# Turned value sums, softmax rows divided on ScalarE, and no turning step for the outputs, in a hybrid attention and expert layer

## The reference

```python
n = rms_norm(x)                                # width 1024
fq, fk, fv, ff, sq, sk, sv, ga, gb = split(n @ w_in)
# forgetting attention, 8 heads of 64: softmax(q.k/8 + C[t] - C[s]), s <= t
p = softmax(where(valid, s, MASK));  o_fox = p @ fv
# stick-breaking attention, 8 heads of 64, s < t, in log space
a = exp(log_sigmoid(z) + tail);      o_sb = a @ sv
merged = sigmoid(ga) * (o_fox @ w_o_fox) + sigmoid(gb) * (o_sb @ w_o_sb)
h = x + merged @ w_out
out = h + peer_ffn(rms_norm(h))                # 8 heads x 16 experts for a row
```

## Time and profile before

| | before |
|---|---|
| median of 3 runs | 4224.8 us (4221.11 to 4228.86) |
| profiled execution, span | 4221.9 us |
| TensorE busy | 3201.1 us, 76% |
| VectorE busy | 2854.8 us, 68% |
| GpSimd busy | 1367.6 us, 32% |
| ScalarE busy | 1198.4 us, 28% |
| moved by DMA | 1367.21 MB, mean 324 GB/s |

### The profile page before, as it was taken

How to read it: one execution, slowest core, us unless ns; L and a number is a source line. 1 busy time by engine, 2 the same in 40 slices (tenths; PEclk the granted TensorE clock), 3 DMA queues, 4 the chain that set the end, 5 groups by cost and what they waited for, 6 DMA issues and landing times.

```text
span 4221.9 us, 32194 instructions
## 1 busy us (share of the span) xinstructions
PE 3201.1 (76%) x9766; PEld 1661.7 (39%) x9766; DVE 2854.8 (68%) x5552; ACT 1198.4 (28%) x2584; POOL 1367.6 (32%) x1086
## 2 busy tenths in 40 slices
PE   6989918869887677859887759997586677768565
PEld 3345613325445333425454424554262233334222
DVE  2012285778767966768766978886889767467865
ACT  1223102126521112126631116664111245111100
POOL 0000011444433322433333324443434333434463
PEclk9976959878888878978888878998798788878777
DMA  3422346999999958998989888999999888999997
GB/s 122 138 69 102 113 174 229 401 401 384 382 401 380 369 198 304 410 373 353 345 359 392 316 301 347 379 386 383 380 398 364 302 333 339 400 418 384 383 419 324
DMA packets 296027, 1367.21 MB, mean 324 GB/s; under 512 B 36056, under 2 KB 96624, under 8 KB 149392
## 3 DMA queue, kind: packets, MB, share of 16 engines
q0 software_dynamic: 154464, 1116.02, 66.1%
q1 hardware_dynamic: 110480, 222.78, 14.8%
q10 hardware_dynamic: 30912, 26.35, 1.9%
HBM read 1329.52 MB, written 35.10 MB: 323 GB/s over the span
## 4 chain that ended last, share of the span: by engine, by line
DVE 22%; DMA 12%; PE 11%; ACT 5%; issue 5%; SPq 2%; POOL 1%; ACTq 0%; DVEq 0%; POOLq 0%
DVE uv L1365 10%; DMA uv<-expert_uv,rows_u 8%; PE pv L796 5%; DVE held L1388 2%; SPq L537 2%; DVE arena L1356 1%; PE pb L906 1%; DMA uv<-expert_uv,rows_pk 1%; DMA arena<-scratch_gates 1%; POOL uv L699 1%; PE pb L854 1%; PE pb L749 1%; ACT L1140 1%; PE pb L879 1%; DVE arena L1426 1%
## 5 line engine op out<-in xcount | busy, mean ns | idle before, releaser
L699 POOL DMA_INDIRECT uv<-expert_uv,rows_u x1024 | 1311.7, 1281 | 2203.1 <-PE pv L796 1225.8
L796 PE MATMUL pv<-uv,diag 128*128 128x512 f32 x2344 | 1263.8, 696 | 404.2 <-ACT diag L1102 329.5
L1365 DVE CUSTOM_DVE_ANT_0 uv<-uv,nr 128x1024 f32<-128x1024 f32 x1056 | 1240.8, 1220 | 195.5 <-DMA uv<-expert_uv,rows_u 160.9
L796 PEld LDWEIGHTS pv<-uv,diag 128*128 128x128 f32 x2344 | 511.4, 226 | 1062.0 <-issue 984.0
L965 PE MATMUL pb<-arena 128*128 128x512 f32 (+1 forms) x1440 | 651.9, 611 | 35.5 <-ACT arena L1249 35.5
L1388 DVE SCALAR_TENSOR_TENSOR held<-uv,wgt,held 128x1024 f32<-128x1024 f32 x470 | 603.9, 1285 | 16.6 <-DVE wgt L1376 0.3
L1109 ACT ACTIVATE gel<-dots 128x4 f32<-128x4 f32 x264 | 54.2, 205 | 1878.3 <-DVE dots L1365 1810.2
L965 PEld LDWEIGHTS pb<-arena 128*128 128x128 f32 (+1 forms) x1440 | 266.6, 189 | 398.4 <-issue 357.5
L749 PE MATMUL pb<-arena 64*128 64x512 f32 (+6 forms) x544 | 274.1, 621 | 166.2 <-DMA arena<-scratch_c_p 94.2
L778 PE MATMUL pb<-arena 128*128 128x64 f32 (+3 forms) x1728 | 248.7, 290 | 35.2 <-ACT o L1091 35.2
L778 PEld LDWEIGHTS pb<-arena 128*128 128x128 f32 (+3 forms) x1728 | 229.9, 197 | 102.1 <-issue 66.3
(11 more groups left out here) (149 smaller groups left out, 2631.3 us busy)
## 6 DMA issues: line engine op xcount, KB each, us to landing
arena<-w_stream SPq DMA_DIRECT2D x80, 1024.0 KB, 9.3
arena<-w_main SPq DMA_DIRECT2D x60, 1024.0 KB, 9.5
uv<-expert_uv,rows_u POOLq DMA_INDIRECT x1024, 10.9
scratch_gates<-arena ACTq DMA_DIRECT2D x32, 256.0 KB, 9.7
arena<-scratch_gates SPq DMA_DIRECT2D x8, 1024.0 KB, 22.2
o<-x SPq DMA_DIRECT2D x14, 512.0 KB, 15.1
arena<-scratch_c_p SPq DMA_DIRECT2D x8, 520.0 KB, 8.2
arena<-x_t SPq DMA_DIRECT2D x8, 512.0 KB, 5.6
```

The source lines that it names most:

```text
L699: pool.indirect_dma_start(out=uv[k % NU][:].rearrange("p a n -> p (a n)"), out_offset=None, in_=io["expert_uv"][:, :], in_offset=bass.Indi ...
L796: mm = nc.tensor.matmul(pv[:, c * BANK:(c + 1) * BANK], diag[n % ND][:], uv[k % NU][:, 1, c * BANK:(c + 1) * BANK], start=n == first, stop ...
L1365: nc.vector.tensor_tensor_reduce(out=u, in0=u, in1=row[:], scale=1.0, scalar=0.0, op0=ALU.mult, op1=ALU.add, accum_out=dots[b % 2][:, k % ...
```

## The change

The value sums are made turned: V is the stationary side now (64 columns), the turned probabilities are the moving side (a query a column), and the result has the head's 64 dimensions on partitions 0 to 63 or 64 to 127, by the head's number. So `take_output` copies straight into what the output projection reads, now called `o_t`, and the step "outputs" is gone with its transposes and copies. A query is a column then, and can't be divided by a scale of its partition, so the softmax rows are divided in front of the turn, in `probabilities` on ScalarE: exp(-ln(sum)), then a copy of the whole row with that as scale. VectorE's `invert` is gone. On SP's queue, x is loaded after the chunks 4 to 7, when the last output projection has read `o_t`. With the step gone, the planner spreads the same lots over the other steps.

```diff
-    steps = [("outputs",), ("y", 0), ("y", 1), ("merged",), ("h", 0), ("h", 1), ("norm",), ("turned",)]
+    steps = [("y", 0), ("y", 1), ("merged",), ("h", 0), ("h", 1), ("norm",), ("turned",)]
...
-        o = [[o_rows[i][:, k, :] for i in range(2)] for k in range(KINDS)]
+        o_t = [[o_rows[i][:, k, :].rearrange("p (f q) -> p f q", f=PAIRS) for i in range(2)] for k in range(KINDS)]
...
-        po = pb[:, 5, 0:DH]
+        po = pb[:, 5, 0:P]
...
-                    sp.wait_ge(o_turned, tiles[-1] + 1)
-                    for ti, t in enumerate(tiles):
-                        r = query_rows(t)
-                        sp.dma_start(xh[ti][0:r], io["x"][first_row(t):first_row(t) + r, :]).then_inc(x_in[ti], 16)
                     for c in range(NW, 8 + NW):
                         if c == NW + 4:
+                            for ti, t in enumerate(tiles):
+                                r = query_rows(t)
+                                sp.wait_ge(y_ready, 2 * tiles[0] + len(tiles) + ti + 1)
+                                sp.dma_start(xh[ti][0:r], io["x"][first_row(t):first_row(t) + r, :]).then_inc(x_in[ti], 16)
...
-                        mm = nc.tensor.matmul(po[0:r], probt[n % 2][0:w, slot, 0:r],
-                                              vt[k][pair % 2][0:w, slot, hh * DH:(hh + 1) * DH],
-                                              start=j == 0, stop=j == len(blocks) - 1)
+                        mm = nc.tensor.matmul(po[hh * DH:(hh + 1) * DH, 0:r], vt[k][pair % 2][0:w, slot, hh * DH:(hh + 1) * DH],
+                                              probt[n % 2][0:w, slot, 0:r], start=j == 0, stop=j == len(blocks) - 1)
...
-                    def turn_outputs():
-                        pe.wait_ge(o_out, plan.end[g])
...
-                    def project_outputs(c):
-                        pe.wait_ge(ot_out, tiles[-1] + 1)
+                    def project_outputs(c):
+                        pe.wait_ge(o_out, plan.end[g])
...
-                        nc.scalar.activation(p, p, ACT.Exp, scale=-1.0, bias=stat[0:r, i % 2, 0:1],
-                                             accum_out=stat[0:r, i % 2, 1:2]).then_inc(probs, 1)
+                        step(nc.scalar.activation(p, p, ACT.Exp, scale=-1.0, bias=stat[0:r, i % 2, 0:1], accum_out=stat[0:r, i % 2, 1:2]))
+                        step(nc.scalar.activation(stat[0:r, i % 2, 1:2], stat[0:r, i % 2, 1:2], ACT.Ln))
+                        step(nc.scalar.activation(stat[0:r, i % 2, 2:3], stat[0:r, i % 2, 1:2], ACT.Exp, scale=-1.0))
+                        nc.scalar.activation(p, p, ACT.Copy, scale=stat[0:r, i % 2, 2:3]).then_inc(probs, 1)
...
-                    if k == 0:
-                        act.wait_ge(inverted, i + 1)
                     act.wait_ge(summed_up, n + 1)
-                    nc.scalar.activation(o[k][ti][0:r, h * DH:(h + 1) * DH], po[0:r], ACT.Copy,
-                                         scale=1.0 if k else stat[0:r, i % 2, 2:3]).then_inc(o_out, 1)
+                    half = slice(hh * DH, (hh + 1) * DH)
+                    nc.scalar.activation(o_t[k][ti][half, hp, 0:r], po[half, 0:r], ACT.Copy).then_inc(o_out, 1)
...
-                def take_outputs():
...
-                def invert(n):
...
-                    nc.vector.reciprocal(stat[0:r, i % 2, 2:3], stat[0:r, i % 2, 1:2]).then_inc(inverted, 1)
```

More of the change, by code:

```diff
@@ L316, in stream @@
         o_rows = [sb(f"o{i}", [P, KINDS, WID]) for i in range(2)]
-        o = [[o_rows[i][:, k, :] for i in range(2)] for k in range(KINDS)]
+        o = [o_rows[i][:, 0, :] for i in range(2)]
+        o_t = [[o_rows[i][:, k, :].rearrange("p (f q) -> p f q", f=PAIRS) for i in range(2)] for k in range(KINDS)]
         xh = [o_rows[i][:].rearrange("p k n -> p (k n)") for i in range(2)]
@@ L431, in stream @@
         minimum, magnitude, exponent = sem("minimum"), sem("magnitude"), sem("exponent")
-        probs, inverted = sem("probs"), sem("inverted")
+        probs = sem("probs")
         turned, turned_out = sem("turned_b"), sem("turned_b_out")
@@ L440, in stream @@
         chunk_used = sem("chunk_used")
-        o_turned, ot_out = sem("o_turned"), sem("ot_out")
         y_ready, merged = sem("y_ready"), sem("merged")
@@ L831, in merge @@
                     chunk = lambda c: chunk_no(g, 2 * COLS + c)
-                    def turn_outputs():
+                    def project_outputs(c):
                         pe.wait_ge(o_out, plan.end[g])
-                        for ti, t in enumerate(tiles):
-                            r = query_rows(t)
-                            if ti:
-                                pe.wait_ge(ot_out, t)
-                            for k in range(KINDS):
-                                for f in range(4):
-                                    mm = nc.tensor.transpose(pturn[:, k * 4 + f, 0:r], o[k][ti][0:r, f * P:(f + 1) * P], ident[0:r, 0:r])
-                            mm.then_inc(o_turned, 1)
-                    def project_outputs(c):
-                        pe.wait_ge(ot_out, tiles[-1] + 1)
                         for k in range(KINDS):
@@ L853, in project_outputs @@
                                 for f in range(4):
-                                    mm = nc.tensor.matmul(pb[0:r, ti * 2 + k, :], ot[:, k * 4 + f, ti * P:ti * P + r],
+                                    mm = nc.tensor.matmul(pb[0:r, ti * 2 + k, :], o_t[k][ti][:, f, 0:r],
                                                           wring[n % NW][:, f * BANK:(f + 1) * BANK], start=f == 0, stop=f == 3)
@@ L926, in merge @@
                     for s, step in enumerate(merge_steps(tiles)):
-                        if step[0] == "outputs":
-                            turn_outputs()
-                        elif step[0] == "y":
+                        if step[0] == "y":
                             project_outputs(step[1])
@@ L1144, in merge @@
                     width = sum(query_rows(t) for t in tiles)
-                    def take_outputs():
-                        for ti, t in enumerate(tiles):
-                            r = query_rows(t)
-                            act.wait_ge(o_turned, t + 1)
-                            nc.scalar.activation(ot[:, :, ti * P:ti * P + r], pturn[:, :, 0:r], ACT.Copy).then_inc(ot_out, 1)
                     def take_merged():
@@ L1187, in merge @@
                         ahead(("merge", g, s))
-                        if step[0] == "outputs":
-                            take_outputs()
-                        elif step[0] == "merged":
+                        if step[0] == "merged":
                             take_merged()
@@ L1327, in mark @@
                     return count[0]
-                def invert(n):
-                    g, pair, cki, hp, hh, t, ti, tj, k = plan.units[n]
-                    if k:
-                        return
-                    r, i = query_rows(t), plan.kind_no[n]
-                    dve.wait_ge(probs, n + 1)
-                    nc.vector.reciprocal(stat[0:r, i % 2, 2:3], stat[0:r, i % 2, 1:2]).then_inc(inverted, 1)
                 def exponents(n):
@@ L1410, in attend @@
                         inside = 0 <= s < units
-                        if 0 < s <= units:
-                            invert(n0 + s - 1)
                         if 0 <= s + 1 < units:
```

## The result

| | before | after |
|---|---|---|
| median | 4224.8 us (4221.11 to 4232.03) | 4250.7 us (4246.84 to 4251.64) |
| ratio, 95% interval | | 1.0058, 1.0044 to 1.0072 |
| profiled execution, span | 4221.9 us | 4247.8 us |

The changed kernel is 26 us slower, in the medians as in the two spans. Forecast were 4.5 us, with 4219 to 4239 as the forecast's own range and 4206 to 4260 as the whole one. 4250.7 lies in the whole range, 12 us above the forecast's own.

A forecast was written before the change was run, and what follows sets the result against it. No engine is full, so the wait ending last in each stage bounds the kernel. Terms 14 + 3 + 5 - 4 - 1.5 - 12 = +4.5 us on 4224.8 gave about 4229, own range 4219 to 4239, whole range 4206 to 4260.

The forecast's parts named there:

- rival 1: ScalarE's chain gates the waves with lots too, half of its 78 us paid: +34, 4263 us, chance 0.13.
- What bounds: No engine full; wave 0's loop passes on every microsecond; in merges the weight chunk is late next, VectorE waits for gates.
- Wave 0's attention, +14 and +3: Wave 0: division chain delays the output copy, 0.9 us per softmax unit, +14; 64-column value-sum loads on TensorE, +3.
- The chain in waves 1 to 4, +5 and -4: Attentions with lots: division chain mostly covered by the wait for dots, +5 us; VectorE's reciprocal gone, -4.
- The merges, -1.5 and -12: Turning step gone: wave 0's merge -1.5 us; waves 1 to 4, sooner projections and moved lots, -12 (0 to -30).
- Value sums in waves 1 to 4, counted as nothing: Attentions with lots: the forecast's sum had no cost for the turned value sums' new shape on TensorE.
- Rival 3: TensorE pays for the shape change in every unit, also with lots: +13, 4242 us, chance 0.14.
- x: Residual rows loaded after the last output projection: costs nothing, or +5 us a wave if the cover is gone.
- Rival 2: Merge steps come forward by the whole turning step, gates included: -14, 4215 us, chance 0.20.
- Rival 4: Granted clock in wave 0's attention goes from 0.50 to 0.81: -25, 4204 us, chance 0.05.
- Rival 5: The load of x in its new place isn't hidden: +25, 4254 us, chance 0.05.

The follow-up runs named there:

- e8: Changed kernel without the softmax division and with the lots in their old places: +10.9 us against the kernel before, ratio 1.0025.
- e3: Changed kernel without the softmax division, Exp alone left: -7.6 us against the kernel before, ratio 0.9980.
- e2: Kernel before with the softmax rows divided on ScalarE and no scale in the output copy: +22.2 us against the kernel before, ratio 1.0043.
- e4: Changed kernel with the output copy of unit s-2 ahead of the probabilities of unit s: -10.9 us against the kernel before, ratio 0.9967.
- e11: Changed kernel without division, lots in old places, plus a dummy turning step whose result nothing reads: +9.7 us against the kernel before, ratio 1.0023.
- e1: Changed kernel with an empty outputs step, so lots stand in their old places: +37.1 us against the kernel before, ratio 1.0085.
- e6: Kernel before with the outputs step's share at 0, so lots stand as in the changed kernel: -13.2 us against the kernel before, ratio 0.9964.
- e5: Kernel before with the output copy of unit s-2 ahead of the probabilities of unit s: -11.6 us against the kernel before, ratio 0.9971.
- e10: Kernel before with the output copy first and lots moved only in waves before 3: -31.5 us against the kernel before, ratio 0.9927.
- e7: Changed kernel with the output copy first and old lot places in waves 3 and 4: -14.3 us against the kernel before, ratio 0.9969.
- e9: Kernel before with the output copy first and lots placed as in the changed kernel: -26.1 us against the kernel before, ratio 0.9941.
- e12: Changed kernel without division and with the output copy first: -12.7 us against the kernel before, ratio 0.9963.

## Why the prediction came out as it did

**The number.** The terms made +4.5 and 25.9 was measured. That 4250.7 lies in the range is owed to the range's width: its upper part belonged to rival 1 (4263, chance 0.13, and itself 3 us outside the range that was to end with it). By terms, from e8, e3 and the changed kernel: wave 0's attention +18.4 for +17. The chain in waves 1 to 4 +18, for +1 with the reciprocal. The turned value sums outside wave 0's attention, with the step gone, +8, for nothing. The lots' new places -18.5, where the merges and the lots were to give -13.5 together.

**What bounds.** Right for wave 0: every microsecond of its loop arrived. It was right that the chunk is late next behind the turns (2937.08 in the chain of wave 3, 5.4 us of idle time at the first output projection of wave 0). That VectorE's merge still waits for the gates is half right: it does in waves 1 and 4, but not in wave 3, where the projection that waited for the chunk comes last now.

**Wave 0's attention, +14 and +3.** Both right in mechanism and size: e2 gives 14.1, and e3 and e8 give 3.1. The parts are right too: 0.20, 0.20, 0.41 (for 0.40) and 0.52 (for 0.50), and 1162 ns for 1150. That it is right to a tenth is luck. The output copy starts 1.04 us later behind its Exp, not 0.9: the reading of the sum (0.18 us) now stands ahead of the Ln, which starts 0.52 after the Exp's start where the output copy started 0.39 after. From e3 to after it is 15.3. The wait for the output copy was to be about 20 us and is 23.1; the stage was to take 132 and takes 133.5. The +3 was the middle between two bounds. The Trainium skill, "TensorEngine Tiling (Array Packing)", Key Properties, has TensorE drained when the tiling mode changes. The upper end that I took for this, 6 us, is not reached in wave 0: it is 3.1, and 4.8 with the output copy first.

**The chain in waves 1 to 4, +5 and -4.** The +5 is the first term that was mis-sized. It is +8 in e2 (22.2 less wave 0's 14.1), and 18 between e3 and after (33.5 less 15.3), where by attentions wave 1 has 11.6, wave 2 5.6, wave 3 1.7, wave 4 2.5. The GELU's wait for dots in wave 3 was to fall from 94.7 us to about 70, and fell to 84.9:

```profile
ACT gel L1095 <- DVE dots L1335: 84.9, 31, 7.5
```

So the cover held in waves 3 and 4. Waves 1 and 2 have the five softmax units each without a lot, and it is their price that was too low. I had named these steps and counted 0.3 to 1 us for each. The value sums' waits for the output copy show what they cost; wave 1 in the changed kernel, then in e3:

```profile
PE pb L778 <- ACT o L1078: 19.6, 8, 5.9
```

```profile
PE pb L778 <- ACT o L1076: 13.0, 8, 3.5
```

In wave 2 it is 14.4 for 8.1. The two differences make 12.9 us in ten such units, 1.3 us each: the chain in full, at these widths, as in wave 0. That is 12.9 of the 17.2 us by which the two attentions differ; where the rest goes isn't shown. With the copy first (e4) wave 1's attention is 12.6 us shorter than after's, wave 3's 0.1 longer. The reciprocal's -4 can't be seen apart from the rest.

**The merges, -1.5 and -12.** Wave 0's -1.5 was -1.1. The -12 has about the size of what the lots gave (-11 to -18), for the wrong reason: that is luck. I had put 4 us into each of waves 1 and 2 for a sooner projection together with the lot in the hole, and 2 into waves 3 and 4. The step that failed is that a sooner projection shortens the merge. In e8 wave 2's projection starts 4.8 us sooner, and nothing of it is left at the projection by w_out, 2 us later than with the turns in e11. In the changed kernel itself it starts only 1.3 us sooner: TensorE waits 9.6 us for the chunk, which I had taken to land after 4.9. What the rows said against it, I had read: the gates stand behind four chunks in SP's queue. I took their earlier landing as a maybe; none came. The whole gain is the lots: from e1 to after 10 and 11 us in waves 1 and 2, 8 lost in wave 3 and 2 in wave 4. Waves 3 and 4 were forecast as a gain of 2 each. That a lot fits into the hole behind the projection is in the last stage window (27.7 us of VectorE's 34). But 5 and 10 us of waves 1 and 2's gain (4 and 5 in e6) are in the attention, which has 23 lots before and after; these stand at other steps, and why that takes 4 to 10 us off isn't shown.

**Value sums in waves 1 to 4, counted as nothing.** The second mis-sized term. With no lot moved and no chain, all outside wave 0's attention costs 7 to 8 us more than before (e8: 10.9 less 3.1; e11: 9.7 less 3.1). Wave 4's attention is the part on which the kernels agree. With the lots in their old places it is at -1.4 to +2.8 with the old value sums (e2, e5, e10) and at +4.6 to +7.8 with turned ones (e1, e7, e8, e11); with moved lots at +3.2 and +3.7 (e6, e9) and at +11.0 to +13.5 (after, e3, e4, e12). It goes with the clock (below). Rival 3 had this sign. It put 13 us on top of the forecast's 3 for the value sums' shape (its own terms make 14); 10 in all were measured, and not evenly: the attentions of waves 1 to 3 changed by +3.6 in sum in e8 and by -0.9 in e11.

**x.** Right: nothing. VectorE's addition is released by TensorE all 16 times (67.4 us, 64.0 in 15 waits before), and x is in no wait of a merge; the one wait of the kernel for a load of x is at its start, 10.2 us for 10.3.

**The rivals.** Rival 1 came nearest: the chain gates waves 1 and 2, with 8 to 18 of the 78 us, not half, and not because the wait for dots was gone in wave 3. Rival 2 fell with e8 and e11. For rival 3 see above. Rival 4: wave 0 stayed at a granted clock of 0.50. Rival 5 fell.

## What to carry to other kernels

Before an instruction chain is put on an engine, look at what stands behind it in that engine's order and who waits for that. Here 37 us hung on whether a 0.3 us copy stood before or behind a chain of 1.0 us, and the same turn of order gained 12 us in the kernel before. A step that is taken out gives only what the next late thing leaves. Where loads stand behind it, a dummy in its place tells its price in one run. And when a planner shifts work because a step is gone, run that shift by itself (here -13 us): its gain belongs to the shares, and can be had without the change. Last, price a thin cover at the full cost: the steps that had none paid the whole chain.

## What the runs showed of the hardware

**The granted clock of wave 4's attention.** It has the fewest queries a unit (32). Stretch, length, busy us and instructions of TensorE, its loads, VectorE, ScalarE, GpSimd, then granted clock, DMA share and GB/s; waves 2 and 4 before:

```profile
1861.00:2173.00 312.00, 271.63 (x1004) 159.09 (x1004) 246.05 (x362) 189.90 (x395) 113.08 (x91) 0.82 0.87 338
3341.00:3599.00 258.00, 200.13 (x810) 90.38 (x809) 177.46 (x253) 128.19 (x272) 85.79 (x74) 0.78 0.84 318
```

The same two after:

```profile
1873.00:2180.00 307.00, 268.30 (x1004) 145.49 (x1004) 241.90 (x340) 213.69 (x445) 120.69 (x94) 0.85 0.92 355
3359.00:3631.00 272.00, 220.86 (x822) 100.65 (x822) 178.61 (x247) 142.44 (x300) 96.10 (x78) 0.74 0.83 309
```

Wave 4 with old value sums, output copy first and lots moved (e9), then with turned value sums, no chain, lots in their old places and dummy turns (e11):

```profile
3318.00:3580.00 262.00, 203.27 (x824) 92.09 (x824) 178.82 (x255) 129.36 (x277) 95.01 (x78) 0.79 0.85 323
```

```profile
3339.00:3605.00 266.00, 217.22 (x812) 98.86 (x810) 176.19 (x244) 128.83 (x272) 92.01 (x74) 0.73 0.82 308
```

The granted clock of wave 4's attention is 0.77 to 0.80 in all six kernels with the old value sums (before, e2, e5, e6, e9, e10), and 0.73 to 0.75 in all eight with turned ones. It is a mean over the stretch of two levels, 1.2 and 2.4 GHz, so more of the stretch ran at the lower one. The background matmuls of the experts, whose code is the same, pay for it there: 696 ns each before, 747 after (line, shapes and count; busy us, mean ns; idle before):

```profile
L796 PE MATMUL pv<-uv,diag 128*128 128x512 f32 x220 | 118.1, 696 | 4.0 <-DVE held L1395 4.0
```

```profile
L795 PE MATMUL pv<-uv,diag 128*128 128x512 f32 x232 | 135.5, 747 | 5.4 <-DVE held L1365 4.3 <-ACT diag L1088 1.1
```

In waves 1 and 2 it does not fall: wave 1 has 0.81 before and 0.82 after, wave 2 0.82 and 0.85. What TensorE did differently in wave 4 is that V, with 64 columns, is loaded and 32 columns are moved, where 32 were loaded and 64 moved. That this is the cause of the lower grant was not tried, nor whether the lower grant makes wave 4 longer or only comes with it; a kernel with turned value sums in waves 0 to 3 alone would tell.

**A load that isn't pulled ahead.** In wave 0 the value sum stands behind the mask matmul. With the old value sums its load follows the mask's load at once (e5):

```profile
332.09 0.10 PEld L753 LDWEIGHTS pb<-masks,ident_b 128*128 128x128 bf16 x1 [0.70 <-issue]
332.10 1.14 PEld L778 LDWEIGHTS pb<-arena 128*128 128x128 f32 x4
```

With 64 columns, no chain and the same order (e12) it comes 0.21 us behind it:

```profile
332.12 0.10 PEld L753 LDWEIGHTS pb<-masks,ident_b 128*128 128x128 bf16 x1 [0.70 <-issue]
332.33 0.71 PEld L778 LDWEIGHTS pb<-arena 128*64 128x64 f32 x4
```

Over the 32 units the starts of mask matmul and value sum lie 3.4 us apart in e5 and 6.6 in e12. That is 3.2 of the 4.8 us between these two kernels in wave 0's attention; the passes themselves add 1.0. In wave 0 of the kernel before, TensorE's loads for value sums idle 6.1 us in 14 of them, 18.2 in 49 in e3, none for longer than 0.6.

In wave 1, at a granted clock of 0.81 before and 0.82 after, the value sum of a unit takes 0.09 us longer (1.14 to 1.23 us for eight passes), though the passes follow each other no more slowly (112 ns before, 110 after).
